# Unread identity products on TensorE in front of ten waits of a two-block transformer step

## The reference

```python
# even layer: rotated queries and keys, attention over the top 64 keys
q = apply_rope(rmsnorm(heads(q), q_norm_g), cos_a, sin_a)
k = apply_rope(rmsnorm(heads(k), k_norm_g), cos_a, sin_a)
# odd layer: per chunk of 64 tokens and head
decay = jnp.exp(jnp.where(tril, g[..., :, None] - g[..., None, :], -jnp.inf))
m = jnp.where(strict, jnp.einsum('bhncd,bhnsd->bhncs', kb, k) * decay, 0.0)
t_inv = lax.linalg.triangular_solve(eye + m, ..., lower=True, unit_diagonal=True)
# mixer
hx = modulate(x, norm1_g[i], sh1, sc1)          # rms norm, scale and shift
px_all = hx @ w_in[i]
# routing and experts: each of 16 experts takes its 32 best tokens
aff = jax.nn.softmax(jnp.einsum('bnd,de->bne', h, w_router), axis=-1)
g, idx = lax.top_k(aff.transpose(0, 2, 1), cap)
xs = jax.vmap(lambda hb, ib: hb[ib])(h, idx)
y = jnp.einsum('becf,efd->becd', jax.nn.silu(xs @ w_gate) * (xs @ w_up), w_down)
```

## Time and profile before

| what | value |
|---|---|
| median of 3 runs | 2300.99 us |
| lowest, highest | 2299.65, 2302.06 us |
| the profiled execution | 2306.43 us |
| its span in the profile | 2304.4 us |
| PE busy (matmuls) | 1902.8 us, 83% |
| DVE, ACT busy | 929.3 us, 685.2 us |
| mean granted TensorE clock | 0.927 |

### The profile page before, as it was taken

One profiled execution on the slowest core, in us unless ns is written; L12 is line 12 of the kernel. 1 busy time (PEld: TensorE's weight loads), 2 busy tenths in 40 slices (PEclk: granted clock), 3 DMA queues, 4 the chain that ended last, 5 costly groups with the idle time before them and its releaser, 6 DMA issues.

```text
span 2304.4 us, 30197 instructions
## 1 busy us (share of the span) xinstructions
PE 1902.8 (83%) x13320; PEld 1376.3 (60%) x13320; DVE 929.3 (40%) x1596; ACT 685.2 (30%) x1090; POOL 4.1 (0%) x11
## 2 busy tenths in 40 slices
PE   7799999888898999878989888878767876565666
PEld 5489999878777999866774333323255743232322
DVE  5766666667665665654431110101065511010101
ACT  4345544543524544444322100000044310000000
POOL 0000000000000000000000000000000000000000
PEclk9999999899998999989989999999988988788878
DMA  6664445441467435412226999999922689999997
GB/s 248 232 243 170 183 162 186 156 163 57 183 224 277 179 136 195 183 39 110 110 110 287 427 428 429 427 427 429 427 107 110 254 345 426 427 427 427 427 427 323
DMA packets 44787, 606.52 MB, mean 263 GB/s; under 512 B 5105, under 2 KB 5233, under 8 KB 6769
## 3 DMA queue, kind: packets, MB, share of 16 engines
q1 hardware_dynamic: 43488, 597.61, 63.7%
q0 software_dynamic: 880, 4.98, 0.6%
q10 hardware_dynamic: 288, 2.02, 0.2%
HBM read 603.54 MB, written 1.05 MB: 262 GB/s over the span
## 4 chain that ended last, share of the span: by engine, by line
PE 53%; DMA 27%; DVE 13%; ACT 6%; issue 2%; SPq 0%; DVEq 0%; ACTq 0%
PE ps L85 52%; DMA m_more<-moe_up 10%; DMA m_ring<-moe_up 5%; DMA m_ring<-moe_down 3%; DVE m_WL L94 2%; DMA m_moe_sc<-moe_gate 2%; DMA m_side_slot<-moe_down 2%; DMA m_more<-moe_down 1%; DMA m_ring<-moe_gate 1%; DMA m_more<-moe_gate 1%; ACT m_WH L91 1%; ACT m_mix_sc L91 1%; DVE m_od_low L100 1%; PE ps L88 1%; DMA m_ring<-ev_in 1%
## 5 line engine op out<-in xcount | busy, mean ns | idle before, releaser
L94 DVE TENSOR_TENSOR m_WL<-m_ring,m_WH 128x1024 fp32r<-128x1024 f32 (+1 forms) x277 | 329.8, 1201 | 271.1 <-ACT m_WH L91 270.4
L85 PE MATMUL ps<-m_more,m_moe_sc 128*32 128x256 f32 (+1 forms) x1648 | 319.1, 542 | 85.3 <-DMA m_more<-moe_up 52.9
L91 ACT ACTIVATE m_WH<-m_ring 128x1024 fp32r<-128x1024 f32 (+1 forms) x277 | 282.4, 1034 | 137.2 <-PE ps L85 124.9
L85 PE MATMUL ps<-m_ring,m_moe_sc 128*32 128x256 f32 (+1 forms) x1104 | 247.7, 552 | 52.4 <-DMA m_ring<-moe_up 26.9
L85 PEld LDWEIGHTS ps<-m_more,m_moe_sc 128*32 128x32 f32 (+1 forms) x1648 | 118.6, 142 | 234.0 <-issue 116.5
L85 PE MATMUL ps<-m_nH,m_WH 128*128 128x256 f32 x936 | 236.7, 289 | 19.3 <-ACT m_WH L91 19.3
L85 PE MATMUL ps<-m_nL,m_WH 128*128 128x256 f32 x936 | 236.4, 289 | 8.8 <-DVE m_nL L100 8.7
L85 PEld LDWEIGHTS ps<-m_nH,m_WH 128*128 128x128 f32 x936 | 182.4, 195 | 23.1 <-ACT m_WH L91 21.1
L85 PEld LDWEIGHTS ps<-m_nL,m_WH 128*128 128x128 f32 x936 | 182.5, 195 | 12.5 <-DVE m_nL L100 11.6
L85 PEld LDWEIGHTS ps<-m_ring,m_moe_sc 128*32 128x32 f32 (+1 forms) x1104 | 91.0, 144 | 144.8 <-issue 76.5
L91 ACT ACTIVATE m_moe_sc<-ps 32x512 f32<-32x512 f32 (+3 forms) x86 | 40.2, 473 | 390.1 <-PE ps L85 378.9
(11 more groups left out here) (307 smaller groups left out, 3149.4 us busy)
## 6 DMA issues: line engine op xcount, KB each, us to landing
m_more<-moe_up SPq DMA_DIRECT2D x37, 2048.0 KB, 26.7
m_more<-moe_gate SPq DMA_DIRECT2D x33, 2048.0 KB, 26.6
m_more<-moe_down SPq DMA_DIRECT2D x29, 2048.0 KB, 23.6
m_ring<-moe_gate SPq DMA_DIRECT2D x26, 2048.0 KB, 25.3
m_ring<-moe_down SPq DMA_DIRECT2D x25, 2048.0 KB, 26.7
m_ring<-ada SPq DMA_DIRECT2D x24, 2048.0 KB, 7.5
m_ring<-moe_up SPq DMA_DIRECT2D x22, 2048.0 KB, 25.2
m_ring<-ffn_down SPq DMA_DIRECT2D x16, 1408.0 KB, 6.0
```

What stands on the lines that cost most here:

```text
L85: return Issued() if self.dry else self.e.matmul(out, lhsT, rhs, start=start, stop=stop, skip_group_check=skip)
L91: return Issued() if self.dry else self.e.activation(*a, **k)
L94: return Issued() if self.dry else self.e.tensor_tensor(*a)
```

## The change

A new method of the bank ring tells which bank the next `take` will give, without taking it. A new helper writes n products into it: the 128x128 fp32 identity as weights, and as moving operand the same identity seen four times (512 columns of fp32). Each starts and ends its own accumulation and signals nothing; the next real group that takes the bank overwrites it.

```diff
+    def idle(self):
+
+        b = self.places[self.n % len(self.places)]
+        before = self.read.get(b)
         return self.banks[b], (self.at(before) if before else (None, 0))
...
+        def pe_warm(n):
+
+            ps, before = fg.idle()
+            pe.wait_ge(*before)
+            for _ in range(n):
+                pe.matmul(ps[:, :].rearrange("p (k t) -> p k t", k=4), ident, bc(ident.unsqueeze(1), [128, 4, 128]), True, True)
...
             pe_jobs.until(jobs[1])
             pe_jobs.fill(1)
+            pe_warm(20)
             for t in range(2):
                 pe_transposes(("qT", t), block4(eq, t), ["q turned"], fg, ("qT out", t))
...
                         *P.mark(("decay", H, t)))
+                if H == 0:
+                    pe_warm(12)
                 for t in range(2):
                     pe_transposes(("knT", H, t), ...
...
             for side in (1, 0):
+                if side == l:
+                    pe_warm(11 if l else 13)
                 pe_stats(("mix", l, side), acc[side], [previous(l, side)])
...
+            pe_warm(21)
             run(pe_tokens(("kv", l), "w_in", (l,), 8, mxH, mxL, both, hr, lr, fg))
...
             pe_jobs.fill(2)
+            if l:
+                pe_warm(9)
             for s in range(2):
                 pe_transposes(("mkT", l, s), ...
...
                 pe_jobs.fill(1)
+                if l:
+                    pe_warm(10)
                 for t in range(2):
                     pe_transposes(("mqT", l, s, t), ...
...
             ins.then_inc(*P.mark(("affT", l)))
+            pe_warm(12)
             ps, before = fg.take(("places", l), ("hot", l, last))
...
             ins.then_inc(*P.mark(("places", l)))
+            pe_warm(5)
             for side in range(nside):
```

More of the change, by code:

```diff
@@ L138, in take @@
         self.of[group] = self.banks[b]
+        return self.banks[b], (self.at(before) if before else (None, 0))
+    def idle(self):
+        b = self.places[self.n % len(self.places)]
+        before = self.read.get(b)
         return self.banks[b], (self.at(before) if before else (None, 0))
```

## The result

| | before | after |
|---|---|---|
| median of the runs beside each other | 2301.52 us (4 runs, 2299.65 to 2302.12) | 2334.71 us (4 runs, 2333.2 to 2338.28) |
| ratio after / before | | 1.0148 (95% interval 1.013 to 1.0165) |
| the profiled execution | 2306.43 us | 2334.1 us, span 2332.8 us |
| mean granted TensorE clock | 0.927 | 0.948 |

The change costs 33.2 us (29.9 to 38.0 by the interval); the forecast was +39.4, 2340.4 us, with a range of 2322 to 2353. The clock rose as intended and the kernel is slower all the same. (The title counts ten waits; eleven of the twelve calls stand in front of one, and the odd layer's call stands in front of none.)

A forecast was written before the change was run, and what follows sets the result against it. PE was taken to bound most of the time up to the expert loops, loads the loops, whose start depends on PE. Products' time less waits less clock gains summed to +39.4 on 2301.0: 2340.4 us, range 2322 to 2353.

The forecast's parts named there:

- The price of a product: All twelve calls: one product is two records, 0.86 us at full clock, so 151 products take 130 us of PE.
- the rival of products that don't keep the clock: All calls: clock falls despite the products, each costs up to 1.72 us, nothing won; +189, 2490 us; chance 0.03.
- that of the cheap product: All calls: a product takes 0.43 us, nearly all calls end inside their waits; -9.3, 2291.7 us; chance 0.06.
- The odd layer, read as a call in front of no wait: Call behind the decay products: 10.3 us covers only 1.2 before `kk`, nothing won; +9.1, bounds 4 and 10.3.
- a late expert loop stays late: Expert loops: loads set the pace but start when PE frees a slot, so PE's lateness delays the loop equally.
- The steps of mixer 0: Mixer 0's statistics and `kv`: products overrun their waits, less what the warm clock wins; +3.8 and +5.7.
- mixer 1: Statistics, `kv`, `mkT`, `mqT`: overruns less what the warm clock wins; +2.5, +4.5, +0.6, +0.8.
- The even layer, "I take +2.7": Even layer's 20 products: DVE's low part comes 2.7 us late and releases the next load; +2.7, bounds 0 and 4.8.
- Routing 0, "I take 5 us, which costs 2.5": Routing 0's first call starts at the low level for 5 us, costing 2.5; with the overrun +6.9.
- Routing 1's second call, "0": Selection matrices of routing 1: overrun of 1.45 us balanced by 1.5 won from the clock; 0.
- The rival of absorbed delays: DVE and ACT absorb even layer, odd layer and half the mixers' overruns; +19.3, 2320.3 us; chance 0.06.

The follow-up runs named there:

- the fitted kernel: The change without the odd layer's call, other counts cut to fit their waits, 71 products: 2287.36 us, ratio 0.9943; on another occasion 2290.57 us, 0.9956.
- the filled one: the fitted kernel with `kv` 13, even layer 11, routing 0's places 6, six new before `TT`, 83 products: 2286.37 us; again 2288.12 us.
- the kernel with transposes: the fitted kernel with each product replaced by eight transposes of the 128x128 identity: 2290.62 us, ratio 0.9954.

## Why the prediction was right, and where its sum was too high

**What held.** The price of a product, 0.86 us and two records, was 0.87. The waits of the earlier trace rows in front of the calls vanished and the clock behind them is 1.00, so the rival of products that don't keep the clock is out, and so is that of the cheap product: with the count unchanged, half the columns took 45 us off. That the calls are too long for their waits is shown by the fitted kernel, which has 71 products and is 10 to 14 us faster than before, and 39 us faster than the 139 products in the same eleven places. The odd layer, read as a call in front of no wait, measured +9.0 at `kk` against 9.1, and +7.5 us (4.4 to 10.8) by itself. That a late expert loop stays late is shown by the load, 29.8 us later. The steps of mixer 0 (6.7 to 15.6 at 1028 us, +8.9; the forecast had 3.8 + 5.7 = 9.5) and of mixer 1 (17.2 at the experts to 25.6 at `affT`, +8.4; the forecast had 2.5 + 4.5 + 0.6 + 0.8 = 8.4) came out as worked out. The exactness of the last is luck: kernels without a call in that stretch move there by up to 2.8 us.

**What failed**, all of it terms that were sized too high:
- *The even layer, "I take +2.7".* It is +0.3 to +0.5 (kernel with that call alone), near its own lower bound of 0. DVE's low part was late as foreseen (2.4 us); the 2.7 were taken for lasting because a load is released by it. But that load came in 1.2 us faster than before, and PE won 0.7 behind it; PE's own waits up to 193 us shrank from 8.0 to 4.7. The step that failed is adding a lateness to a load's end as if the load always took the same time, and carrying it past the next 100 us without reading the waits there.
- *Routing 0, "I take 5 us, which costs 2.5".* The low start did not occur in the profile of the change, and where it occurs the low level lasted 2.2 us or less in the call, not 5, in the profiles read here; that is 1.1 us. The earlier trace rows was one execution of two possible ones. The call cost 4.2 in the trace instead of 6.9, and the pair at most +2.7 instead of +5.3.
- *Routing 1's second call, "0".* It measured -1.5: +1.0 at the first gathering product, then 1.1 won in the gathering, where the forecast had 1.5 from the clock of 0.79, and 1.4 between the start of the expert loop and the last product. Why the loop gave back 1.4 isn't settled.

Summed by the table from 53 us on, the calls cost 28.4 + 2.2 = 30.6 us in the trace: even layer and what lies up to the decay products -0.8, odd layer 9.0, 0.7 in between, mixer 0 8.9, -1.1 in the stretch that runs high or low by chance, routing 0 2.7, mixer 1 8.4, routing 1 2.8. The medians say 33.2. The profiled execution of before lay 5 us above its median, which is enough for the difference; a part of that may be the chance stretch, in which it had fallen to the low level.

**The rival of absorbed delays** said that even layer, odd layer and half the mixers' overruns vanish. One of its three parts came true, the even layer's. The odd one didn't, nor those of the mixers. (Its 8.3 is half of the statistics' and `kv` terms alone; with `mkT` and `mqT` half of the mixers' is 9.0.)

## What to carry to other kernels

Products that keep TensorE's clock up pay only inside a wait: here 71 fitted ones won 10 to 14 us, 139 in the same places lost some 25, and 12 more without a wait another 8. Count them by a duration read from a row of the same type and width (here 0.86 us, two records of an fp32 product), divide the wait by it and stay below; a little too short cost nothing that the runs could tell, while products too many cost their length wherever PE was what the next stretch waited for (odd layer, mixers, places). In the even layer, where DVE and a load were, 7.5 us too many cost 0.5. Look at the idle time on the very instruction behind the call: a call 23 us ahead of the wait it is meant for fills nothing.

## What the runs showed of the hardware that was not expected

- The granted clock in a stretch of one-column and 16-column products differs between two executions of the same program: 1.00 in one, falling to 0.50 in the other, in the fitted kernel and in the filled one alike. In the fitted one it differs so in four other places too.
- Transposes hold the clock as fp32 products do: 80 in a row at 0.11 us each, 1.00 in them and behind them.
- Idle rests of 1.6 and 2.5 us in front of the two `kv` were followed by 0.76 and 0.52 in the fitted kernel. A rest of 2.4 us in front of routing 0's places was followed by 1.00 there, and by 0.77 over 7 us in the kernel with transposes.
- Eight products at the start raised the clock for about 3 us only.
- Filling the last rests brought the clock to 1.00 at both `kv` and `TT`, and no time that the runs could tell from none. At both `kv` DVE is busy for nearly the whole window (6.96 and 6.80 of 7.00 us), so a faster PE may only meet it there; at `TT` it is busy for 5.25, and the reason stays open.
